# In the woven half, TensorE adds a pick two slabs behind its dot product instead of three

## The chip, the cores and the metric

One core of one Trainium2 chip. Five engines work from their own instruction queues and meet in semaphores: PE (TensorE, the matrix multiplier), DVE (VectorE), ACT (ScalarE), POOL (GpSimd) and SP (SyncE, which here only issues DMAs). The metric is the device time of one execution in microseconds (us), the median of several runs.

## The reference, cut to what matters

Two transformer blocks over 512 tokens of width 1024, the second one with 16 meta tokens ahead of them. The first block ends in a mixture of very many tiny experts: each token picks 8 heads x 16 = 128 of 16384 experts, and each expert is a row `u` and a row `v`.

```python
def chunk(args):                       # 128 tokens at a time
    hc, ec, gc = args
    u_sel = jnp.take(u, ec, axis=0)
    act = jax.nn.gelu(jnp.einsum('chkd,cd->chk', u_sel, hc), approximate=False) * gc
    v_sel = jnp.take(v, ec, axis=0)
    return jnp.einsum('chk,chkd->cd', act, v_sel)
...
for l in range(DEPTH):                 # the second block
    h = h + 0.5 * swiglu(rmsnorm(h, ffn1_norm[l]), ...)
    h = h + hybrid_mixer(rmsnorm(h, mix_norm[l]), pos, k_top, ...)   # retention and attention
    h = h + 0.5 * swiglu(rmsnorm(h, ffn2_norm[l]), ...)
```

The first 256 tokens of the second block do not need the experts of the last 256 tokens of the first block (everything is causal). The kernel uses this.

## The kernel before, in words

**Slabs.** All weights are streamed in slabs of 128 x 1024 numbers (0.5 MB each). SP loads a slab, ACT rounds it (`slabs_rounded`, L1452), DVE makes the remainder (`slabs_remainder`, L2279), and PE multiplies it in three products of reduced precision (L715), so a slab of 8 tiles is 24 matmuls. The rounded slabs have 4 places. So ACT can round slab t+3 only when PE's first matmul on slab t has ended.

**Picks.** The experts of one tile of 128 tokens are handled as 128 picks. Pick n means: one row of `u` and `v` for each of the 128 tokens. POOL gathers these 128 rows of 8 KB (1 MB, L3259) into one of 6 places (`SLOTS`), DVE takes the dot product of the `u` half with the token (L2578), ACT makes gelu, coefficient and a 128 x 128 diagonal of coefficients (L1742, L1746, L1753), and PE multiplies the diagonal with the `v` half and accumulates in two PSUM banks (`weigh`, L1068, two matmuls, which the profile shows as four). That frees the place for pick n+6. There are 4 tiles, 512 picks.

**Two halves.** Picks 0 to 255 run by themselves (to about 1440 us in the trace). Picks 256 to 511 are woven into the second block's work on its first 272 tokens, which has 261 slabs (`BLOCK2`). In this woven half every third pick is added by DVE in place of PE (`by_dve`, L2734, no diagonal). I count slabs of the woven half with t = 0 to 260. Its stages are: up and gate slabs of the first feed-forward (t = 0 to 43, in pairs), its down slabs (t = 44 to 67, three to an output chunk: 8, 8 and 6 tiles), the index and retention slabs (68 to 128), the retention output (129 to 144), the attention values (145 to 152), the attention heads (153 to 176, three slabs to a head: query, key, gate), the two output projections (177 to 192), then the second feed-forward (193 on).

**What sets the order.** Nothing is scheduled at run time. Each engine's program walks the slabs, and at each slab t it does its share of the picks up to a number that `woven_by` gives:

- `woven_by(t)` is t + 4, and one more for each five slabs of the mixer: about one pick a slab, 1.2 in the mixer.
- DVE, at its step t: the remainder of slab t+3, the dot products up to `woven_by(t)`, its own rows up to `woven_by(t - 2)` (`rows_by`), and only then what it does for the stage itself.
- ACT, at its step t: it rounds slab t+3, then makes gelu, coefficient and diagonal up to `woven_by(t - 1)`.
- PE, ahead of slab t (`slab`): `weigh` up to `added_by(t)`, which before the change is `woven_by(t - 3)`.
- Where PE would wait for DVE in a norm or ahead of an attention head's scores, `fill(2)` and `fill(1)` let it weigh up to `woven_by(t - 2)` or `woven_by(t - 1)` there. They name their own distance, so the default that is changed does not reach them.

PE runs its queue strictly in order. A `weigh` whose diagonal is not ready holds up all that stands behind it. A claim of a PSUM bank stands ahead of the `weigh` of the same slab (`one(x, 0, T, claim(gm))`: the claim is an argument and is worked out first).

**Turns.** `TURN` holds the two slabs at which the sums of a tile of tokens are taken out of PSUM, by DVE at step `TURN[i]` (L2750) and step `TURN[i] + 2` (L2586), by PE at slab `TURN[i] + 2` (`turn_rows`). PE starts the next tile's picks at `TURN[0] + 3`.

Of the kernel before, what the change touches and what calls it, by code (L numbers as in the profile page):

```python
# [181 lines left out]
BLOCK2 = 4 * FT + 2 * 3 * KT + 5 + 12 * RET_HEADS + 6 * KT + 3 * ATT_HEADS  # L182
# [15 lines left out]
def woven_by(t):  # L198

    if t < 0:  # L200
        return 0
    mixing = min(max(t + 1 - UP_AND_DOWN, 0), BLOCK2 - 2 * UP_AND_DOWN)
    return min(WOVEN, t + 4 + mixing // 5)


def turn_after(n):

    return next(t for t in range(BLOCK2) if woven_by(t - 3) >= n)


TURN = (turn_after(PICKS), turn_after(WOVEN))
assert TURN[1] + 4 < BLOCK2, TURN


def added_by(t, behind=3):

    n = woven_by(t - behind)
    return PICKS if n > PICKS and t < TURN[0] + 3 else n
# [115 lines left out]
def build(nc, slabs_d, xT_d, memT_d, metaT_d, vecs_d, consts_d, consts16_d, subk_d, wi_d, peer_uv_d, out_d,  # L334
          n_slabs):
    ctx = ExitStack()
    with ctx:
# [344 lines left out]
        def _(pe):  # L682
# [425 lines left out]
            def fill(behind=2):  # L1108


                if place[0] < BLOCK2:
                    weigh_to(added_by(place[0], behind))
# [9 lines left out]
            def slab():  # L1122

                t = place[0]
                place[0] += 1
                if t < BLOCK2:
                    weigh_to(added_by(t))
                    if t in (TURN[0] + 2, TURN[1] + 2):
                        turn_rows(list(sums_at), [acc.take(), acc.take()])
                return Slab()  # L1130
# [2290 lines left out]
```

## Time and profile before

| | us |
|---|---|
| median of 3 runs | 3600.69 |
| lowest and highest run | 3599.6, 3603.47 |
| the profiled execution, first to last instruction | 3601.5 |
| PE busy, DVE busy, ACT busy | 3316.3, 2554.4, 1537.0 |
| PE idle between 1440 and 2622 us by named waits, largest: the norms' sums (L802) | 14.4 |

The profile gives the profiled execution as its span alone; no other time of it is told, and the span lies inside the spread of the runs. A busy PE is not a PE at its peak: its matmuls overlap, and a matmul's start is shown some 0.4 us early when a pick stands ahead of it. The profile also shows the share of TensorE's clock that the chip granted (PEclk, 1.00 is 2.4 GHz, 0.50 is 1.2 GHz).

### The profile page before, as it was taken

What the parts mean: (1) busy time and instruction counts of PE and PEld (TensorE: products, weight loads), DVE (VectorE), ACT (ScalarE), POOL (GpSimd) and SP (SyncE); (2) the same over time, 40 slices, a digit from 0 to 9 for tenths busy, and PEclk for the clock granted to TensorE, in tenths of its full rate; (3) what the DMA queues carried; (4) which work ended last, traced back from release to release, by engine and by line L of the source; (5) the groups of instructions that cost most, each with busy time, mean ns of one, the idle gap of its engine ahead of it and who ended that gap; (6) DMA issues with size and microseconds to landing.
All of it is one profiled execution on the core that took longest, in us unless ns stands there. A gap on an engine that the chain in (4) does not pass through costs nothing.

```text
span 3601.5 us, 50492 instructions
## 1 busy us (share of the span) xinstructions
PE 3316.3 (92%) x18706; PEld 2633.5 (73%) x18706; DVE 2554.4 (71%) x4532; ACT 1537.0 (43%) x3089; POOL 770.5 (21%) x577
## 2 busy tenths in 40 slices
PE   7998889979898777799999999989999999999998
PEld 6886669855463222688777777767899988998898
DVE  6997143676777877687767777877867576768665
ACT  3222234245443333454444444545445443444443
POOL 1001236123435666122122122222200000000000
PEclk9999999999999999899899999999999999999999
DMA  3332224569999999699888899879956844453455
GB/s 123 94 95 75 75 83 141 182 272 397 407 415 421 417 411 418 261 377 389 324 321 312 305 372 385 317 296 341 374 176 188 267 141 131 133 184 106 140 184 156
DMA packets 184174, 918.82 MB, mean 255 GB/s; under 512 B 21536, under 2 KB 26912, under 8 KB 118128
## 3 DMA queue, kind: packets, MB, share of 16 engines
q0 software_dynamic: 73728, 536.90, 37.4%
q1 hardware_dynamic: 99248, 358.66, 29.9%
q10 hardware_dynamic: 10960, 20.12, 1.8%
q8 instruction: 145, 2.38, 0.3%
q14 instruction: 93, 0.76, 0.1%
HBM read 907.80 MB, written 7.80 MB: 254 GB/s over the span
## 4 chain that ended last, share of the span: by engine, by line
PE 72%; DVE 9%; DMA 7%; issue 5%; ACT 4%; POOL 2%; ACTq 0%; DVEq 0%; POOLq 0%
PE psum L715 54%; PE psum L1068 11%; DMA buffer_float<-in_peer_uv,buffer_uint 7%; DVE buffer_bfloat L2578 2%; POOL buffer_float L3259 2%; PE psum L1289 1%; ACT slabs_rounded L1452 1%; PE psum L723 1%; DVE buffer_float32r L2185 1%; PE psum L1274 1%; DVE norm_recip_root L2193 1%; DVE slabs_remainder L2279 1%; PE psum L1286 1%; PE psum L1372 1%; PE psum L1336 1%
## 5 line engine op out<-in xcount | busy, mean ns | idle before, releaser
L715 PE MATMUL psum<-buffer_float32r,slabs_rounded 128*128 128x256 f32 (+2 forms) x9568 | 2005.4, 309 | 70.3 <-POOL slabs_remainder L3244 30.1
L715 PEld LDWEIGHTS psum<-buffer_float32r,slabs_rounded 128*128 128x128 f32 x9568 | 1556.1, 192 | 217.3 <-issue 113.5
L715 PE MATMUL psum<-buffer_float32r,slabs_remainder 128*128 128x256 f32 (+2 forms) x4784 | 1439.8, 301 | 0.0
L2279 DVE TENSOR_TENSOR slabs_remainder<-raw_slabs,slabs_rounded 128x1024 fp32r<-128x1024 f32 x601 | 732.8, 1223 | 452.2 <-ACT slabs_rounded L1452 434.1
L1452 ACT ACTIVATE slabs_rounded<-raw_slabs 128x1024 fp32r<-128x1024 f32 x662 | 695.7, 1055 | 698.5 <-PE psum L715 620.7
L1068 PE MATMUL psum<-buffer_float,buffer_float 128*128 128x512 f32 x1712 | 825.2, 612 | 137.8 <-ACT buffer_float L1753 124.5
L715 PEld LDWEIGHTS psum<-buffer_float32r,slabs_remainder 128*128 128x128 f32 x4784 | 918.1, 192 | 29.8
L3259 POOL DMA_INDIRECT buffer_float<-in_peer_uv,buffer_uint x512 | 623.2, 1217 | 1330.8 <-PE psum L1068 753.6
L2578 DVE CUSTOM_DVE_ANT_0 buffer_bfloat<-buffer_float,buffer_float 128x1024 bf16<-128x1024 f32 x512 | 625.3, 1221 | 169.5 <-DMA buffer_float<-in_peer_uv,buffer_uint 160.8
L1068 PEld LDWEIGHTS psum<-buffer_float,buffer_float 128*128 128x128 f32 x1712 | 304.3, 193 | 519.6 <-issue 509.7
L1742 ACT ACTIVATE buffer_float<-buffer_float 128x1 f32<-128x1 f32 x512 | 100.3, 196 | 368.5 <-DVE buffer_float L2578 366.6
L3244 POOL TENSOR_TENSOR slabs_remainder<-raw_slabs,slabs_rounded 128x1024 fp32r<-128x1024 f32 x61 | 147.2, 2425 | 496.4 <-ACT slabs_rounded L1452 496.1
L1753 ACT ACTIVATE buffer_float<-fixed,buffer_float 128x128 f32<-128x128 f32 x428 | 172.1, 402 | 40.6 <-ACT buffer_float L1746 1.9
L715 PE MATMUL psum<-slabs_rounded,buffer_float32r 128*128 128x512 f32 (+1 forms) x608 | 184.2, 388 | 4.0 <-issue 4.0
L1436 ACT ACTIVATE buffer_float32r<-buffer_float 128x256 fp32r<-128x256 f32 (+3 forms) x224 | 104.0, 482 | 134.9 <-DVE buffer_float L2239 44.5
L2323 DVE SCALAR_TENSOR_TENSOR buffer_float<-buffer_float,vecs,buffer_float 128x512 f32<-128x512 f32 x232 | 158.9, 744 | 0.0
L1746 ACT ACTIVATE buffer_float<-buffer_float,buffer_float 128x1 f32<-128x1 f32 x512 | 150.9, 295 | 16.8
L2185 DVE TENSOR_TENSOR buffer_float32r<-buffer_float,buffer_float32r 128x256 fp32r<-128x256 f32 (+2 forms) x224 | 124.1, 568 | 19.8 <-ACT buffer_float32r L1436 18.1
L715 PEld LDWEIGHTS psum<-slabs_rounded,buffer_float32r 128*128 128x128 f32 x608 | 110.7, 190 | 36.4 <-issue 16.4
L715 PE MATMUL psum<-slabs_remainder,buffer_float32r 128*128 128x512 f32 (+1 forms) x304 | 113.3, 373 | 0.0
L2734 DVE SCALAR_TENSOR_TENSOR buffer_float<-buffer_float,buffer_float,buffer_float 128x1024 f32<-128x1024 f32 x82 | 105.0, 1281 | 0.0
L1837 ACT ACTIVATE buffer_float<-psum 128x256 f32<-128x256 f32 (+1 forms) x88 | 34.0, 386 | 103.4 <-PE psum L715 103.4
(213 smaller groups left out, 2039.0 us busy)
## 6 DMA issues: line engine op xcount, KB each, us to landing
raw_slabs<-in_slabs SPq DMA_DIRECT2D x682, 512.0 KB
buffer_float<-in_peer_uv,buffer_uint POOLq DMA_INDIRECT x512
buffer_float<-kept ACTq DMA_DIRECT2D x4, 874.5 KB, 6.0
xT<-in_xT ACTq DMA_DIRECT2D x4, 512.0 KB, 5.7
buffer_float<-in_consts ACTq DMA_DIRECT2D x8, 256.0 KB
kept<-buffer_float ACTq DMA_DIRECT2D x4, 512.0 KB
buffer_float<-kept ACTq DMA_DIRECT2D x2, 875.0 KB, 6.7
kept<-buffer_float ACTq DMA_DIRECT2D x4, 272.0 KB
```

Of the source, the lines that this page charges most:

```text
L715: m = pe.matmul(out, a, b, start=start and j == 0, stop=stop and j == 2)
L1068: m = pe.matmul(psum[:, b, :], diag[:, slot, :], uv_rows[slot][:, D + q * 512:D + (q + 1) * 512], start=p == 0, stop=p == PICKS - 1)
L1452: act.activation(slab_h[:, j, :], raw[:, r, :], ACT.Copy).then_inc(slab_rounded, 1)
L1746: act.activation(coefs[:, slot:slot + 1], acts[:, slot:slot + 1], ACT.Copy, scale=gates[:, tt, p:p + 1])\
L1753: act.activation(diag[:, slot, :], ident[:, :], ACT.Copy, scale=coefs[:, slot:slot + 1])\
L2185: dve.tensor_tensor(dst, src, high.bitcast(F32), ALU.subtract).then_inc(split, 1)
L2279: dve.tensor_tensor(slab_l[:, r, :], raw[:, r, :], slab_h[:, j, :].bitcast(F32), ALU.subtract)\
L2323: step(dve.scalar_tensor_tensor(out=acc, in0=cfp[:, h, t:t + S], scalar=w, in1=acc, op0=ALU.mult, op1=ALU.add))
L2578: dve.tensor_tensor_reduce(dump, uv_rows[slot][:, 0:D], hrow[tt], 1.0, 0.0, ALU.mult, ALU.add, dots[:, slot:slot + 1]).then_inc(dotted, 1)
L2734: ins = dve.scalar_tensor_tensor(out=out_rows, in0=v, scalar=c, in1=out_rows, op0=ALU.mult, op1=ALU.add)
L3244: pool.tensor_tensor(slab_l[:, r, :], raw[:, r, :], slab_h[:, j, :].bitcast(F32), ALU.subtract)\
L3259: pool.indirect_dma_start(uv_rows[slot], None, peer_uv_d, bass.IndirectOffsetOnAxis(eidx[:, tt, p:p + 1], 0))\
```

## The change

PE's distance goes from three slabs to two, in `added_by`, and the two turns are worked out from the same distance.

```diff
 def turn_after(n):

-    return next(t for t in range(BLOCK2) if woven_by(t - 3) >= n)
+    return next(t for t in range(BLOCK2) if woven_by(t - 2) >= n)
...
-def added_by(t, behind=3):
+def added_by(t, behind=2):

     n = woven_by(t - behind)
     return PICKS if n > PICKS and t < TURN[0] + 3 else n
```

`TURN` goes from (118, 230) to (117, 229). The programs of ACT, POOL and SP are the same in both kernels. DVE's differs only in where the turns stand. On PE each `weigh` (L1068) stands one slab earlier, except where a `fill` has put it already.

The start of the woven half on PE. The rows without a sign stand in both kernels; the L715 rows are the matmuls of a slab, L1068 the picks 256 and 257 (buffer 115 and 116 are the places that their rows lie in).

```order
 L715 MATMUL psum<-buffer_float32r,slabs_rounded 128x272 x2
 L715 MATMUL psum<-buffer_float32r,slabs_remainder 128x272
-L715 MATMUL psum<-buffer_float32r,slabs_rounded 128x272 x2
...
-L715 MATMUL psum<-buffer_float32r,slabs_remainder 128x272
 L1068 MATMUL psum<-buffer_float_115,buffer_float_103 128x512 x2
 L1068 MATMUL psum<-buffer_float_116,buffer_float_103 128x512 x2
```

Before, three slabs stand ahead of the first pick, now two: the 16 rows of one slab have gone from ahead of it to behind it.

An attention head on PE, before the change. L1372 ends the head before, the 256-wide L715 rows are the query slab and later the gate slab, the 272-wide ones the key slab, L1353 and L1358 turn the probabilities, and L1336 is the next head's scores. Buffers 111, 112 and 114 are places of picks (438, 439 and 441).

```order
L1372 MATMUL psum<-buffer_float_173,buffer_float_166 128x128
...
L715 MATMUL psum<-buffer_float32r,slabs_remainder 128x256
L715 MATMUL psum<-buffer_float32r,slabs_rounded 128x272 x2
...
L715 MATMUL psum<-buffer_float32r,slabs_remainder 128x272
L1068 MATMUL psum<-buffer_float_111,buffer_float_103 128x512 x2
L715 MATMUL psum<-buffer_float32r,slabs_rounded 128x256 x2
...
L1353 MATMUL psum<-fixed,buffer_float_179 128x128 x3
L1358 MATMUL psum<-fixed,buffer_float_179 16x128 x2
L1068 MATMUL psum<-buffer_float_112,buffer_float_103 128x512 x2
L1068 MATMUL psum<-buffer_float_114,buffer_float_103 128x512 x2
L1336 MATMUL psum<-buffer_float_171,buffer_float_170 128x144
```

The same head after the change:

```order
L1372 MATMUL psum<-buffer_float_173,buffer_float_166 128x128
...
L715 MATMUL psum<-buffer_float32r,slabs_remainder 128x256
L1068 MATMUL psum<-buffer_float_111,buffer_float_103 128x512 x2
L715 MATMUL psum<-buffer_float32r,slabs_rounded 128x272 x2
...
L1068 MATMUL psum<-buffer_float_112,buffer_float_103 128x512 x2
L715 MATMUL psum<-buffer_float32r,slabs_rounded 128x256 x2
...
L1353 MATMUL psum<-fixed,buffer_float_179 128x128 x3
L1358 MATMUL psum<-fixed,buffer_float_179 16x128 x2
L1068 MATMUL psum<-buffer_float_114,buffer_float_103 128x512 x2
L1336 MATMUL psum<-buffer_float_171,buffer_float_170 128x144
```

The first pick has moved from behind the key slab to ahead of it, the second from the fill ahead of the scores to ahead of the gate slab; the fill keeps one of its two.

## Rows read from the trace of the kernel before

**Rows 1.** The top of the page.

```profile
span 3601.5 us, 50492 instructions
```

**Rows 2.** Busy time by stretch: us, PE, PEld, DVE, ACT, POOL, PEclk, DMA share, GB/s.

```profile
1500.00:1660.00 160.00, 159.73 (x1030) 135.38 (x1029) 126.10 (x184) 78.17 (x177) 37.28 (x38) 1.00 0.98 383
2240.00:2390.00 150.00, 136.03 (x775) 106.50 (x774) 124.93 (x241) 86.04 (x185) 30.42 (x29) 0.93 0.80 298
2480.00:2622.00 142.00, 141.01 (x929) 116.83 (x928) 112.61 (x166) 70.21 (x158) 29.54 (x30) 1.00 0.91 350
```

**Rows 3.** Waits of PE, 1440 to 2622 us: total, times, longest.

```profile
PE psum L1068 <- ACT buffer_float L1753: 7.9, 4, 4.0
```

**Rows 4.** Up and gate slabs in order of time (start, us): PE, then ACT.

```profile
1603.17 1.88 PE L1068 MATMUL psum<-buffer_float,buffer_float 128*128 128x512 f32 x4
1604.48 0.81 PE L715 MATMUL psum<-buffer_float32r,slabs_rounded 128*128 128x272 f32 x2
1607.89 0.41 PE L715 MATMUL psum<-buffer_float32r,slabs_rounded 128*128 128x272 f32 x2
1610.89 1.54 PE L1068 MATMUL psum<-buffer_float,buffer_float 128*128 128x512 f32 x3
...
1605.27 1.06 ACT L1452 ACTIVATE slabs_rounded<-raw_slabs 128x1024 fp32r<-128x1024 f32 x1 [3.25 <-PE psum L715]
1606.84 0.41 ACT L1753 ACTIVATE buffer_float<-fixed,buffer_float 128x128 f32<-128x128 f32 x1
```

**Rows 5.** The start of the woven half: PE, then ACT.

```profile
1471.68 0.41 PE L715 MATMUL psum<-buffer_float32r,slabs_rounded 128*128 128x272 f32 x2
1479.49 8.01 PE L1068 MATMUL psum<-buffer_float,buffer_float 128*128 128x512 f32 x12 [4.65 <-DVE buffer_float L2819]
1486.93 0.81 PE L715 MATMUL psum<-buffer_float32r,slabs_rounded 128*128 128x272 f32 x2
...
1472.83 0.40 ACT L1753 ACTIVATE buffer_float<-fixed,buffer_float 128x128 f32<-128x128 f32 x1
1476.91 0.40 ACT L1753 ACTIVATE buffer_float<-fixed,buffer_float 128x128 f32<-128x128 f32 x1
```

**Rows 6.** Down slabs, one output chunk: PE, then ACT.

```profile
1666.90 0.82 PE L715 MATMUL psum<-buffer_float32r,slabs_rounded 128*128 128x272 f32 x2
1669.56 0.41 PE L715 MATMUL psum<-buffer_float32r,slabs_rounded 128*128 128x272 f32 x2
...
1669.26 0.40 ACT L1753 ACTIVATE buffer_float<-fixed,buffer_float 128x128 f32<-128x128 f32 x1
1672.74 0.43 ACT L1817 ACTIVATE buffer_float<-xT 128x272 f32<-128x272 f32 x1 [3.08 <-DVE xT L2833]
1674.63 0.40 ACT L1753 ACTIVATE buffer_float<-fixed,buffer_float 128x128 f32<-128x128 f32 x1
```

**Rows 7.** Attention heads in order of time: PE, ACT, DVE.

```profile
2285.99 0.42 PE L715 MATMUL psum<-buffer_float32r,slabs_rounded 128*128 128x272 f32 x2
2324.92 3.39 PE L1068 MATMUL psum<-buffer_float,buffer_float 128*128 128x512 f32 x4 [2.78 <-ACT buffer_float L1753]
...
2283.09 0.42 ACT L2015 ACTIVATE buffer_float<-buffer_float,buffer_float 128x144 f32<-128x144 f32 x1 [1.81 <-DVE buffer_float L3120]
2285.47 1.28 ACT L1742 ACT_TABLE_LOAD   x1
2286.77 0.20 ACT L1742 ACTIVATE buffer_float<-buffer_float 128x1 f32<-128x1 f32 x1
2287.39 0.41 ACT L1753 ACTIVATE buffer_float<-fixed,buffer_float 128x128 f32<-128x128 f32 x1
2301.68 0.42 ACT L2015 ACTIVATE buffer_float<-buffer_float,buffer_float 128x144 f32<-128x144 f32 x1 [5.54 <-DVE buffer_float L3120]
2355.41 0.42 ACT L2015 ACTIVATE buffer_float<-buffer_float,buffer_float 128x144 f32<-128x144 f32 x1 [4.34 <-DVE buffer_float L3120]
...
2290.35 1.22 DVE L2279 TENSOR_TENSOR slabs_remainder<-raw_slabs,slabs_rounded 128x1024 fp32r<-128x1024 f32 x1
```

**Rows 8.** The last output projection's first pick: PE, with its idle time.

```profile
2414.09 1.95 PE L1068 MATMUL psum<-buffer_float,buffer_float 128*128 128x512 f32 x4
```

**Rows 9.** Waits of DVE, 2060 to 2240 us: total, times, longest.

```profile
DVE buffer_bfloat L2578 <- DMA buffer_float<-in_peer_uv,buffer_uint: 21.7, 17, 4.7
```

## The prediction

> **What bounds the kernel now.** I read the busy time by stretch first, then PE's waits, then the instructions in order of time at each stage of the woven half. The execution spans 3601.5 us [rows 1]. PE is busy without a gap in the feed-forward stretches, 159.73 of 160 us and 141.01 of 142 us, while DVE, the next engine, has a fifth to spare [rows 2]. Only the attention stretch has room: 136.03 of 150 us. So between 1440 and 2622 us the time is PE's work plus PE's idle time plus what it loses at half clock. The change adds and removes no instruction on PE. It can only alter idle time and clock.
>
> Diagonals hardly hold PE up now: 7.9 us in 4 waits [rows 3]. How much slack is there? In the up and gate slabs [rows 4] a slab alone takes 3.0 us (1607.89 to 1610.89). A pick and a slab take 4.7 us (the pick from 1603.17; slab start to slab start is 3.4 plus 1.3), so a pick is 1.7. The slab shown at 1604.48 truly starts 0.4 later, since the pick ahead of it is still running. ACT rounds three slabs ahead at 1605.27, 0.4 us after that true start, and the diagonal made in the same step ends at 1606.84 + 0.41 = 1607.25. That is 2.4 us after the slab began. PE now takes it behind the slab after, three to five us later. After the change PE takes it behind this very slab, at 3.0 us. So of a slack of one slab and a bit, 0.5 us is left, with 0.15 us for the semaphore. Where ACT makes the diagonal in that minimum, nothing is lost. Where something stands between, each us of delay over 0.5 stalls PE, and PE's queue has the weight slabs behind it. The sum is then a search for the places where ACT's diagonal is late.
>
> **The change part by part.**
>
> *Start of the woven half, a gain.* PE reaches the fourth slab and waits 4.65 us for a PSUM bank, then adds three picks at once [rows 5]; they take 7.4 us to 1486.93 in place of 5.2, because this is half clock. With the change these picks stand ahead of the third slab (first piece of order), so ahead of that bank wait. PE is there at 1471.68; the first diagonal ends at 1473.23 (1472.83 + 0.40), the third pick's at 1477.31 (1476.91 + 0.40). It idles 1.7 us for the first and, two picks of 1.7 later, 0.6 for the other, in place of 4.65, then has the slab to do while the bank is emptied. Gain 2.3 us. If the clock also stays up, another 2.2 and some of the next slab, up to 5. Whether it does I can't read; I take 3, bounds 1 and 5.
>
> *Up and gate slabs, second feed-forward: nothing*, bounds -1 and +1, by the 0.5 us above.
>
> *Down slabs, a loss.* Here ACT's step for the first slab of a chunk stands behind the square of the last chunk's output, which waits for DVE [rows 6]. The last slab of a chunk (6 tiles) truly starts at 1666.90 + 0.4 = 1667.3 and ends at 1669.56: 2.3 us. The first diagonal ends at 1669.26 + 0.40, 2.4 us after that start; the second at 1674.63 + 0.40, 7.7 us after it, the square at 1672.74 ahead of it. After the change, from that start: 2.3 us slab, wait to 2.5 for the first diagonal, pick to 4.2, slab to 7.2, wait to 7.9. So 0.2 + 0.65 = 0.85 us in each of 7 chunks: +6. The chain to the second diagonal hangs on the last slab's start, so the wait comes back in every chunk. Bounds 0 (DVE turns out earlier) and +8.5.
>
> *Turn and retention output: nothing.* In 2060 to 2240 us DVE waits 21.7 us for gathers, 17 times [rows 9]: six places are too few for 1.2 picks a slab. A place is now freed a slab earlier, which takes most of that away and makes diagonals earlier. PE however has almost no idle time there to win back, one stall of 4.0 us apart [rows 3]. The gain of about 1 us on that stall meets small new stalls at the groups of four slabs. I take 0, bounds -4 and +4.
>
> *Attention, a loss.* After each head's exponentials ACT must round a slab and load the gelu table before its first diagonal: the exponential starts at 2283.09, the diagonal ends at 2287.39 + 0.41, 4.7 us later [rows 7]. The query slab is done at 2285.99. Before, the key slab followed at once and hid this. Now the pick stands ahead of the key slab (second and third piece of order), and PE stands still 1.9 us. Behind it on PE is the key slab, and behind that on DVE the rotation of the key, the next head's scores and the next exponential. So a loop closes: 4.7 + 0.15 to the diagonal, 1.7 the pick, 0.4 + 1.05 to ACT's next rounding, and then DVE's unbroken work from the remainder at 2290.35 to the next exponential at 2301.68, 11.3 us. That is 19.3 us a head. Now four heads take 72.3 us, 18.1 each (2283.09 to 2355.41). 1.2 us more for a head, and in the head where PE waited already, 2.78 us [rows 7], that wait moves up by a slab and grows to about 5. Five of the heads have a pick ahead of the key slab, one has not. 5 x 1.2 and some 1 more for the head that waits longest: +7. Bounds +2, if the idle 14 us of this stretch [rows 2] take most of it, and +14 (each of five heads longer by the 2.8 us of the long wait).
>
> One rule speaks to this place. The gelu table load takes 1.28 us in the row at 2285.47, and the next instruction starts at its end, 2286.77 [rows 7]. The Trainium skill, ScalarE: Activation LUTs, "What ACT_TABLE_LOAD costs", says that a switch costs about 2.66 us, a load of about 1283 ns and a drain of about 1380 ns. The trace has the load and no drain behind it, so the row decides; by the page the loop would be 1.4 us a head longer, which as an estimate from that page makes the sum 7 us larger.
>
> *Second output projection, a loss.* The pick at 2414.09 starts with hardly any idle time, just as its diagonal is ready [rows 8]. It now stands one slab, 3.0 us, earlier, and the diagonal (made behind a rounding of the merged output that waits for DVE) cannot come sooner. +3, bounds 0 and +3.3.
>
> *Norms:* `fill` has the same picks there: 0. *Second turn:* off PE's path: 0.
>
> Sum: -3 + 0 + 6 + 0 + 7 + 3 = +13 us. On the profiled 3601.5 us that is 3614.5; on the median of the runs, 0.8 lower, 3613.7. I say 3613.5.
>
> **The rivals.**
>
> *It is faster.* The freed place is the mechanism: with it gathers start a slab earlier, dot products and diagonals follow, and the new stalls never show. For it: the 21.7 us of DVE's waits [rows 9] and a DMA share of 0.98 [rows 2]. Against it: outside 2060 to 2240 us the dot product is not what makes a diagonal late, ACT's order is, and that is unchanged. It would leave the start's gain of 3 to 5, and up to 4 at the turn: 3593 us. It decides if DVE's waits for gathers, not ACT's steps, set the late diagonals.
>
> *No difference.* The attention stalls fall on idle time that is there anyway and the down slabs' chain is 0.5 us shorter than I read: -3 + 2 + 2 + 1 = +2, 3603 us. For it: 14 us of idle time in 150 [rows 2].
>
> *Much slower.* New idle time pulls the clock to half in every head. For it: the pick behind the 2.78 us wait took 3.39 us in place of 1.88 [rows 4, 7], which is half clock, and PEclk is 0.93 in this stretch [rows 2]. Each half-clock spell near such a wait doubles a pick and part of a slab, 3 us; five of them make 3628. The Trainium skill, TensorE: Matmul & The Clock Gate, Part 1, says the same in kind: the half rate is what an idle array falls back to, and activity releases it. Against it: in the rows only the longest wait has such a pick behind it, and four of the five new ones are near 1.9 us.
>
> **How the numbers follow.** Forecast 0.55, faster 0.12, no difference 0.18, much slower 0.15. About 7 us, 0.2%, is what a measurement of this kernel can tell from no change. The forecast's own range is its bounds taken together with some cancelling, 3606 to 3622. For 8 in 10 it must reach into the neighbours: 3600 to 3626. Faster by over 0.2% has 0.10, within 0.2% 0.21, slower 0.69.
>
> **What the profile after would show.** PE's waits for diagonals (L1068 on L1753) would grow from 7.9 us to 20 to 30. In the down slabs such a wait comes twice to a chunk, 0.2 and 0.7 us, so that a chunk is 0.85 us longer. In the attention heads it stands ahead of the key slab, and the exponentials lie 19 to 20 us apart. The 4.65 us ahead of the fourth slab are gone. DVE's waits for gathers around 2060 to 2240 us fall well below 21.7. Wrong I am if the down slabs show no waits (then ACT or DVE moves up with PE), or if the heads keep 18.1 us.

## The result and the profile after

| | before | after |
|---|---|---|
| median, us | 3600.69 | 3664.3 |
| lowest and highest of 5 runs | 3595.22, 3603.47 | 3661.72, 3668.86 |
| span of the profiled execution | 3601.5 | 3659.6 |

The ratio is 1.0182, with a 95% interval of 1.017 to 1.0194. The change costs 63.6 us, where I had forecast 13 and given 26 as the upper end. The direction was right and the size five times too small.

PE's waits ahead of picks, from 1440 us to the end of the woven half (1440 to 2680 us here), answer to [rows 3]. The first line is the waits for a diagonal, the second a wait for a sum bank at the turn. The columns are total, times, longest:

```profile
PE psum L1068 <- ACT buffer_float L1753: 66.6, 49, 8.1
PE psum L1068 <- DVE xT L2586: 3.6, 1, 3.6
```

The waits for a diagonal were 7.9 us in 4 times. So 58.7 us of new waits stand against a span that is 58.1 longer. The two are not the same thing: other waits shrink, so PE's idle time as a whole grows by 50.2 us, and the other 7.9 us are busy time (3324.2 us in place of 3316.3, in part picks at half clock, as below). The larger part of the loss is PE at rest ahead of picks whose diagonal is not there. The mean granted clock is the same in both executions (0.970 and 0.971). The busy time by stretch answers to [rows 2]. The second row is moved to where the same slabs now lie; the third keeps its 142 us and ends near the same slab:

```profile
1500.00:1660.00 160.00, 155.62 (x988) 130.37 (x988) 123.99 (x180) 76.28 (x174) 36.68 (x36) 1.00 0.96 373
2277.00:2441.00 164.00, 136.48 (x768) 105.92 (x767) 123.81 (x238) 86.40 (x185) 27.91 (x28) 0.92 0.73 265
2542.00:2684.00 142.00, 134.75 (x889) 111.97 (x889) 109.01 (x162) 67.61 (x153) 30.27 (x27) 1.00 0.88 334
```

PE was busy for 159.73 of 160 us in the first and 141.01 of 142 in the third; now it rests 4.4 and 7.3 us in stretches to which I had given nothing. PEclk is within 0.01 of before in all three.

The loss is made in every stage. This table is worked out from the starts of the slabs' first L715 matmuls; PE idle counts waits over 0.1 us. Each column is one execution; among the kept executions of the kernels below, stages that an edit does not touch differ by up to 3 us.

| slabs t | stage | us before, after | PE idle before, after | forecast | came |
|---|---|---|---|---|---|
| -3 to 3 | start of the weave | 421.5, 418.6 | 98.4, 96.8 | -3 | -2.9 |
| 3 to 44 | up and gate | 170.9, 175.7 | 0.3, 4.4 | 0 | +4.8 |
| 44 to 68 | down | 102.8, 113.5 | 1.9, 8.0 | +6 | +10.7 |
| 68 to 116 | index, retention | 282.0, 287.6 | 12.2, 18.3 | none made | +5.6 |
| 116 to 126 | turn | 62.8, 75.2 | 4.0, 12.5 | 0 | +12.4 |
| 126 to 153 | retention output, values | 125.8, 132.0 | 0.0, 6.6 | 0 | +6.2 |
| 153 to 177 | attention heads | 149.7, 164.4 | 13.3, 25.6 | +7 | +14.7 |
| 177 to 193 | output projections | 87.7, 90.0 | 9.9, 12.1 | +3 | +2.3 |
| 193 to 232 | second feed-forward | 158.3, 166.7 | 2.9, 9.6 | 0 | +8.4 |

Behind slab 232 some 3 us come back. Up to slab 232 the time grows by 62.2 us and PE's idle time by 51.0.

What holds the late diagonals? I followed each one from t = 3 on (waits over 0.1 us, one of them for another ACT result) back through ACT's unbroken work to the wait at its head: 49 picks, 66.1 us.

| ACT's unbroken work begins with | picks | us |
|---|---|---|
| the rounding of a slab that had not landed (L1452 behind DMA) | 22 | 21.4 |
| a head's exponential (L2015, waits for DVE) | 7 | 20.5 |
| other work of the stage: squares, roundings, roots, value copies | 13 | 10.8 |
| in the turn, a dot product behind ACT's wait for the stores of keys | 1 | 8.1 |
| the rest | 6 | 5.3 |

*An unlanded slab.* PE, then ACT, in the up and gate slabs, in order of time (start, us, the instruction, its idle time and who ended it), against [rows 4]:

```profile
1555.59 0.81 PE L715 MATMUL psum<-buffer_float32r,slabs_rounded 128*128 128x272 f32 x2
1560.87 1.96 PE L1068 MATMUL psum<-buffer_float,buffer_float 128*128 128x512 f32 x4 [1.71 <-ACT buffer_float L1753]
...
1558.76 1.06 ACT L1452 ACTIVATE slabs_rounded<-raw_slabs 128x1024 fp32r<-128x1024 f32 x1 [3.56 <-DMA raw_slabs<-in_slabs]
1560.33 0.40 ACT L1753 ACTIVATE buffer_float<-fixed,buffer_float 128x128 f32<-128x128 f32 x1
```

The slab begins at 1555.59 + 0.4. In [rows 4] ACT rounded 0.4 us after that. Here it stands idle until 1558.76, since the slab three ahead has not landed, and the diagonal behind that rounding ends 4.7 us after PE's slab began instead of 2.4. PE rests 1.71 us. How often ACT waits so, before (1440 to 2622 us) and after (1440 to 2680):

```profile
ACT slabs_rounded L1452 <- DMA raw_slabs<-in_slabs: 49.4, 29, 3.6
```

```profile
ACT slabs_rounded L1452 <- DMA raw_slabs<-in_slabs: 80.5, 32, 6.0
```

The kernel before had 29 such waits, up to 3.6 us, and only one reached PE, by 0.33 us (at 2348.59), because a whole slab lay between the diagonal and its use. In the up and gate slabs (1485 to 1660 us) these waits have also grown, from 11.7 us in 8 (2.6 the longest) to 29.1 in 11 (3.8).

*A down slab*, against [rows 6], PE, then ACT:

```profile
1672.44 0.81 PE L715 MATMUL psum<-buffer_float32r,slabs_rounded 128*128 128x272 f32 x2
1676.41 1.95 PE L1068 MATMUL psum<-buffer_float,buffer_float 128*128 128x512 f32 x4 [0.40 <-ACT buffer_float L1753]
...
1673.97 0.43 ACT L1817 ACTIVATE buffer_float<-xT 128x272 f32<-128x272 f32 x1 [3.07 <-DVE xT L2833]
1675.87 0.40 ACT L1753 ACTIVATE buffer_float<-fixed,buffer_float 128x128 f32<-128x128 f32 x1
```

The square stands ahead of rounding and diagonal as forecast, and costs 0.4 us where I had worked out 0.65. But it is late in only three chunks. In four others the rounding waits for a landing, 0.86 to 1.40 us each at PE.

*A head*, against [rows 7], PE, then ACT:

```profile
2322.67 0.48 PE L715 MATMUL psum<-buffer_float32r,slabs_rounded 128*128 128x256 f32 x2
2328.11 1.96 PE L1068 MATMUL psum<-buffer_float,buffer_float 128*128 128x512 f32 x4 [2.36 <-ACT buffer_float L1753]
...
2323.27 0.42 ACT L2015 ACTIVATE buffer_float<-buffer_float,buffer_float 128x144 f32<-128x144 f32 x1 [0.67 <-DVE buffer_float L3120]
2324.59 1.05 ACT L1452 ACTIVATE slabs_rounded<-raw_slabs 128x1024 fp32r<-128x1024 f32 x1
2325.65 1.28 ACT L1742 ACT_TABLE_LOAD   x1
2327.57 0.40 ACT L1753 ACTIVATE buffer_float<-fixed,buffer_float 128x128 f32<-128x128 f32 x1
2404.55 0.41 ACT L2015 ACTIVATE buffer_float<-buffer_float,buffer_float 128x144 f32<-128x144 f32 x1 [4.48 <-DVE buffer_float L3120]
```

From exponential to the end of the diagonal it is 4.7 us, as read. The four heads of [rows 7] take 81.3 us (2323.27 to 2404.55), 20.3 each, against 18.1 before and 19.3 forecast. Of the seven picks that PE waits for in the heads, four then run at about half clock, 3.5 to 3.8 us in place of 1.9; before it was one. That is the mechanism of the *much slower* rival, at four picks.

*The turn*, PE, then ACT:

```profile
2107.09 1.89 PE L1231 MATMUL psum<-buffer_float,fixed 128*128 128x256 f32 x8
2117.06 3.75 PE L1068 MATMUL psum<-buffer_float,buffer_float 128*128 128x512 f32 x4 [8.09 <-ACT buffer_float L1753]
...
2112.34 1.06 ACT L1452 ACTIVATE slabs_rounded<-raw_slabs 128x1024 fp32r<-128x1024 f32 x1 [11.37 <-DMA kept<-buffer_float]
2115.89 0.20 ACT L1742 ACTIVATE buffer_float<-buffer_float 128x1 f32<-128x1 f32 x1 [1.14 <-DVE buffer_float L2578]
```

ACT waits 11.37 us for the stores of the retention keys (`kept_ret`, L1960). They were issued at 2099.89 to 2100.73, behind two gathers of 2096.25 and 2097.49. The dot product follows the rounding, the diagonal follows that, and PE rests 8.09 us.

### The profile page after: what moved, and what is told of

It is laid out like the page before. It is cut to its first block, busy times and chain, and to the rows that moved or that the text cites. A ratio compares the mean times of both kernels' runs of the same rounds, so it can differ in the third digit from the quotient of the medians.

```text
span 3659.6 us, 50480 instructions
## 1 busy us (share of the span) xinstructions
PE 3324.2 (91%) x18706; PEld 2630.5 (72%) x18706; DVE 2556.5 (70%) x4532; ACT 1536.0 (42%) x3089; POOL 768.9 (21%) x577
## 4 chain that ended last, share of the span: by engine, by line
PE 63%; DMA 13%; DVE 10%; ACT 6%; issue 5%; POOL 2%; ACTq 0%; DVEq 0%; POOLq 0%
PE psum L715 46%; PE psum L1068 10%; DMA buffer_float<-in_peer_uv,buffer_uint 6%; DMA raw_slabs<-in_slabs 6%; DVE buffer_bfloat L2578 3%; ACT slabs_rounded L1452 2%; POOL buffer_float L3259 2%; PE psum L1289 1%; DVE buffer_float32r L2185 1%; ACT buffer_float L1753 1%; PE psum L723 1%; PE psum L1274 1%; DVE norm_recip_root L2193 1%; DVE buffer_float L2239 1%; ACT buffer_float L1746 1%
## 5 line engine op out<-in xcount | busy, mean ns | idle before, releaser
L715 PE MATMUL psum<-buffer_float32r,slabs_rounded 128*128 128x256 f32 (+2 forms) x9568 | 2005.4, 309 | 66.3 <-POOL slabs_remainder L3244 30.1
L715 PEld LDWEIGHTS psum<-buffer_float32r,slabs_rounded 128*128 128x128 f32 x9568 | 1553.6, 192 | 218.3 <-issue 117.2
L715 PE MATMUL psum<-buffer_float32r,slabs_remainder 128*128 128x256 f32 (+2 forms) x4784 | 1437.7, 301 | 0.0
L1452 ACT ACTIVATE slabs_rounded<-raw_slabs 128x1024 fp32r<-128x1024 f32 x662 | 695.8, 1056 | 796.9 <-PE psum L715 689.9
L1068 PE MATMUL psum<-buffer_float,buffer_float 128*128 128x512 f32 x1712 | 837.8, 619 | 198.0 <-ACT buffer_float L1753 182.7
L715 PEld LDWEIGHTS psum<-buffer_float32r,slabs_remainder 128*128 128x128 f32 x4784 | 915.4, 191 | 29.6
L1068 PEld LDWEIGHTS psum<-buffer_float,buffer_float 128*128 128x128 f32 x1712 | 305.5, 194 | 588.7 <-issue 586.2
L1753 ACT ACTIVATE buffer_float<-fixed,buffer_float 128x128 f32<-128x128 f32 x428 | 172.0, 402 | 40.6 <-ACT buffer_float L1746 1.9
L715 PE MATMUL psum<-slabs_rounded,buffer_float32r 128*128 128x512 f32 (+1 forms) x608 | 182.6, 386 | 1.0 <-issue 1.0
L715 PEld LDWEIGHTS psum<-slabs_rounded,buffer_float32r 128*128 128x128 f32 x608 | 109.8, 188 | 32.1 <-issue 12.4
L715 PE MATMUL psum<-slabs_remainder,buffer_float32r 128*128 128x512 f32 (+1 forms) x304 | 112.6, 370 | 0.0
```

What stands on the lines that cost most here:

```text
L715: m = pe.matmul(out, a, b, start=start and j == 0, stop=stop and j == 2)
L1068: m = pe.matmul(psum[:, b, :], diag[:, slot, :], uv_rows[slot][:, D + q * 512:D + (q + 1) * 512], start=p == 0, stop=p == PICKS - 1)
L1452: act.activation(slab_h[:, j, :], raw[:, r, :], ACT.Copy).then_inc(slab_rounded, 1)
L1753: act.activation(diag[:, slot, :], ident[:, :], ACT.Copy, scale=coefs[:, slot:slot + 1])\
```

## The experiments

Times are medians; the kernel before ran beside each set at 3599.2 to 3600.7 us. Two theories were to be told apart. **S:** a diagonal two slabs behind its dot product is made in ACT's step of the slab just ahead, and whatever stands in that step reaches PE. **G** (and its relative **F**): the places come free earlier, so gathers start earlier, and they crowd or reorder the transfers.

### Is the loss made on the spot?

`e1_near_ffn`, distance 2 only for the start and the first feed-forward:

```diff
-def added_by(t, behind=3):
+def added_by(t, behind=None):

-    n = woven_by(t - behind)
+    n = woven_by(t - (behind or (2 if t < 68 else 3)))
```

> The kernel before, with distance 2 for the slabs t < 68 alone (the start of the woven half and the first FFN), 3 behind them, and the turns where they were. In the traces the changed kernel's slab 68 starts 12 us later than before's (107 us less 95 of delay gathered). Theory P (the loss is made place by place, where a pick waits for its diagonal): 3611 to 3614. Rival R (slabs behind give a delay back, because a late TensorE lets the transfers get ahead): 3601 to 3605.

(The bracket in it is a slip; 12 us is what was meant.) Measured 3613.97 us, ratio 1.0039 (1.0026 to 1.0051): 14 us slower. By stage: up and gate 175.5, down 115.9, then every stage as before within 2 us (index and retention 282.0, heads 149.9). The time lies at the upper end of theory P's range.

`e2_near_heads`, the same edit with `2 if 153 <= t < 177`:

> The kernel before, with distance 2 in the 24 slabs of the attention heads alone (t = 153 to 176). The traces have the heads 14.7 us longer in the changed kernel. Theory P (made on the spot): 3612 to 3617. Rival R (the heads were longer only because the transfers came to them late, from the many slabs at distance 2 ahead of them): 3601 to 3606.

Measured 3615.63 us, ratio 1.0045 (1.003 to 1.0059). The heads take 161.3 us in place of 149.7, all else up to slab 232 stays within 2. Theory P holds in both: each of these stages makes its own loss, and the stages behind do not give it back.

### Do the earlier gathers do it?

`e3_gathers_held`, the changed kernel, with POOL held to the old timing:

```diff
                     pool.wait_ge(uv_used[slot], turn)
+                if n >= PURE + SLOTS:
+                    pool.wait_ge(slab_used, BLOCK1 + used_before(n - SLOTS - PURE) + 1)
...
+def used_before(k):
+    return next(t for t in range(BLOCK2) if added_by(t, 3) > k)
```

> The changed kernel, with each gather of the woven half held until TensorE has passed the slab at which the kernel before would have freed its place. TensorE still adds at distance 2, but no gather starts earlier than before. Theory G (the earlier gathers crowd out the slab loads, which are the larger part of the loss): ScalarE's waits for slab landings in the up and gate slabs fall from 29 back to about 12 us, and the time to 3605 to 3630. Theory D (the diagonal is simply not ready two slabs behind, whatever the transfers do): 3655 to 3668, with TensorE's waits for diagonals unchanged.

Measured 3655.73 us, ratio 1.0147 (1.0123 to 1.0171). PE's waits for diagonals and ACT's for landings, 1440 to 2675 us (its lines lie 5 later):

```profile
PE psum L1073 <- ACT buffer_float L1758: 61.7, 43, 6.4
```

```profile
ACT slabs_rounded L1457 <- DMA raw_slabs<-in_slabs: 50.6, 21, 4.9
```

ACT's waits for landings are back at 50.6 us from 80.5 (before: 49.4), yet only 8.6 us of the time come back (the two intervals just meet). Theory G has its effect right, but most of the loss is not that effect. The hold has a price of its own, too: one dot product comes late behind a held gather, and PE rests 5.0 us for it, at 1491.9. Behind that place the up and gate slabs cost nothing: PE is busy for 159.49 us of 1500 to 1660, where it was 159.73 before and 155.62 in the changed kernel, and ACT's waits for landings there are 7.9 us in place of 27.5. Over all stages 12 late diagonals stand behind a landing, for 11.4 us, in place of 22 for 21.4. So about half of what late landings cost comes from the gathers that start earlier.

`e9_diag_late` goes at theory S from the other side. PE stays at distance 3, gathers and dot products stay; ACT alone makes coefficients and diagonals one step later.

```diff
-                    coefficients(woven_by(t - 1))
+                    coefficients(woven_by(t - 2))
...
 def rows_by(t):
-    n = woven_by(t - 2)
+    n = woven_by(t - 3)
...
-            def fill(behind=2):
+            def fill(behind=3):
```

> The kernel before: TensorE adds at distance 3 and frees the places when it did, and the dot products stand where they stood, but ScalarE makes the coefficients and diagonals one step later, one slab ahead of their use in place of two; VectorE's rows one slab later with them, and the fills between the stages at distance 3. Theory S (what costs is that a diagonal is made in ScalarE's step of the slab just ahead: rounding, coefficient and diagonal then have to fit into one slab without its pick, 3.0 us): about the changed kernel's loss, 3645 to 3675, and TensorE's waits for diagonals as there. Rival F (what costs is the nearness of the gather and its dot product, or the earlier freeing): 3598 to 3615.

Measured 3690.89 us, ratio 1.0245 (1.023 to 1.0261). Waits of PE, 1440 to 2705 us:

```profile
PE psum L1068 <- ACT buffer_float L1753: 86.0, 50, 6.8
PE psum L1068 <- DVE buffer_float L2819: 9.3, 4, 5.2
```

A loss like that of the change, and larger than I expected (90 us; the rows and fills moved with it, and what they add isn't separated), without one gather started earlier. Theory F gave at most 3615 and is out. What costs is the one step between ACT's diagonal and PE's use of it, but not at every place: slabs 116 to 126 take 65.0 us here, against 62.8 before and 75.2 in the changed kernel, so the turn's loss is not made by this step alone. Elsewhere this kernel is the longer one: by 7.4 us in the down slabs, 6.8 behind the turn, 5.4 in the heads and 9.2 in the output projections.

### Is it the rounding ahead of the diagonal?

`e4_diag_first`, the changed kernel, ACT's step turned round:

```diff
-                if BLOCK1 + t + 3 < SLABS:
-                    split_ahead()
                 if t < BLOCK2:
                     coefficients(woven_by(t - 1))
+                if BLOCK1 + t + 3 < SLABS:
+                    split_ahead()
```

> The changed kernel, with ScalarE's step turned round: in each step the coefficients and diagonals come ahead of the rounding of the slab three ahead. Theory A (the diagonal is late because it stands behind a rounding that waits for a slab's landing): TensorE's waits for diagonals fall from 60 us to under 20 in the woven slabs and the time to 3605 to 3635. Rival (the diagonals wait for their gathers' dot products, or the rounding takes the diagonal's place as the late one): 3650 to 3675, with the waits moved to the slab's own.

Measured 3712.26 us, ratio 1.0303 (1.0283 to 1.0324), the slowest of all. My theory A fell in this form. Its rival named the right cause, dot products, but gave 3675 at most. ACT's waits, 1440 to 2730 us:

```profile
ACT buffer_float L1742 <- DVE buffer_float L2579: 434.8, 207, 4.6
ACT slabs_rounded L1452 <- DMA raw_slabs<-in_slabs: 1.5, 1, 1.5
```

The waits for landings are all but gone. In their place ACT stands 434.8 us for dot products (7.0 us in the changed kernel), and rounds late. The rounding has to stay where it is, since DVE's step begins with the remainder that needs it and makes the dot product only then.

### How much is landings?

`e10_light_near` halves the bytes of each gather in the woven half. The rows that it leaves are stale, so the last two tiles of tokens are summed from wrong rows. `e11_light_before` is the same edit of the kernel before.

```diff
-                pool.indirect_dma_start(uv_rows[slot], None, peer_uv_d,
+                pool.indirect_dma_start(uv_rows[slot] if n < PURE else uv_rows[slot][:, 0:D], None,
+                                        peer_uv_d if n < PURE else peer_uv_d.rearrange("n (two d) -> (n two) d", two=2),
```

> The changed kernel with half the bytes in each gather of the third and fourth query tile (0.5 MB in place of 1 MB; the value halves of the rows are left as an earlier gather left them, so the last two query tiles are summed from wrong rows). It is read against the next run, the kernel before with the same lightening. Theory L (about a third of the loss comes from slab loads that land late behind the gathers, which ScalarE's rounding waits for ahead of the diagonal: 22 of the 49 late diagonals, 21 us): the two differ by 30 to 42 us in place of 62, and no diagonal is late behind a landing. Rival (landings only happen to be the last of several things that are late): they differ by 55 to 65.

> The kernel before with the same lightening of the gathers, control of the run above. TensorE does not wait for a transfer in the woven slabs at distance 3, but its picks ahead of the weave and the start of it wait for gathers: 3560 to 3600, the same saving at either distance being taken out by the comparison.

Measured 3633.37 and 3592.4 us. They differ by 41.0 us, where the full kernels differ by 63.6: 22.6 us of the loss go with the transfers, by the intervals some 8 us more or less. ACT's waits for landings in the lightened changed kernel, 1440 to 2655 us, and PE's for diagonals:

```profile
ACT slabs_rounded L1452 <- DMA raw_slabs<-in_slabs: 5.4, 3, 2.6
```

```profile
PE psum L1068 <- ACT buffer_float L1753: 42.7, 25, 5.7
```

No late diagonal stands behind a landing any more. Up and gate take 169.5 us (170.5 in the other lightened kernel), the second feed-forward 157.9 (158.3): in these two stages nothing of the loss is left. In the down slabs 6.5 us are left, in the turn 13.5 and in the heads 17.4. Theory L holds, and its 22.6 us fit the 21.4 that I had counted from the trace.

### The heads

`e13_eight_slabs`, the changed kernel, with `behind or (3 if t in (158, 160, 163, 166, 169, 172, 173, 175) else 2)`:

> The changed kernel, with distance 3 at eight slabs of the attention heads alone (t = 158, 160, 163, 166, 169, 172, 173, 175), those whose pick waits 20.5 us in all for a diagonal behind ScalarE's copies of the turned probabilities. Theory H (these eight points make the heads' loss): the heads fall from 164 to about 152 us, the time to 3648 to 3655. Rival (the pick moved to the next slab waits there as long): 3660 to 3668.

(L2015 is the exponential; "copies" in that text is wrong.) Measured 3650.94 us, ratio 1.0151 (1.0133 to 1.0168). The heads take 149.1 us, the kernel before's 149.7. PE's waits for diagonals in them, 2275 to 2430 us, were 20.5 us in 7:

```profile
PE psum L1068 <- ACT buffer_float L1753: 4.0, 4, 2.8
```

Distance 3 at eight slabs brings back 13.4 us (11.8 if each kernel is set against the kernel before that ran beside it). Theory H holds.

### The turn

`e7_turn_only` and `e8_turn_late` swap the turns alone: `turn_after` with `woven_by(t - 2)` in the kernel before, and with `woven_by(t - 3)` in the changed one.

> The kernel before at distance 3, with the two turns one slab earlier (117 and 229) and nothing else. The changed kernel's trace has slabs 116 to 126 12.4 us longer; in them ScalarE stands 11.4 us for the stores of the retention keys, which were issued 2.4 us behind two gathers. Theory T (the turn's place sets when the gathers start that the stores stand behind): 3608 to 3614. Rival (the turn's place is nothing, the 12 us come from distance 2): 3600 to 3604.

> The changed kernel at distance 2, with the two turns at 118 and 230 as before. Theory T as in the run above: 3648 to 3656, ScalarE's wait for the stores under 4 us. Rival: 3660 to 3668, with that wait still over 8 us.

Measured 3600.34 us, ratio 0.9997 (0.9986 to 1.0007), and 3658.39 us, ratio 1.017 (1.0155 to 1.0186). The turn's place alone costs nothing that the times show. At distance 2 it is worth some 6 us by the medians, though the intervals overlap; slabs 116 to 126 take 67.8 us with the turn late, and 75.2 and 75.9 in two kernels with it early. So both of my either-ors were too simple. With the turn late ACT has no wait for the stores, but PE still waits 6.9 us for the next diagonal, behind a root that waits for DVE (L1874); it is the pick that waits 4.0 us in the kernel before. The early turn does put the wait for the stores in, alone too (2040 to 2140 us of the kernel with the turn alone):

```profile
ACT slabs_rounded L1452 <- DMA kept<-buffer_float: 7.7, 1, 7.7
PE psum L1068 <- ACT buffer_float L1753: 3.1, 1, 3.1
```

At distance 3 the spare slab takes up most of it.

`e15_turn_at_3` is the changed kernel with `3 if 116 <= t < 126 else 2`, turns early:

> The changed kernel, with distance 3 in slabs t = 116 to 125 alone, the turns still at 117 and 229. Slabs 116 to 126 are 12.4 us longer in the changed kernel. If distance 2 makes that on the spot: those slabs at 63 to 67 us and the time 3650 to 3656. If it comes from the order of the gathers and the stores of the keys, set by the turn's place and by what is in flight before slab 116: 72 to 76 us, and 3660 to 3667.

Measured 3650.3 us, ratio 1.014 (1.0123 to 1.0156), those slabs 63.7 us. So the turn's loss needs distance 2 in these slabs; the place of the turn changes which diagonal is late, and some of the size.

### A version with the distance by place

`e6_near_start`: `2 if t < 5 else 3`.

> The kernel before, with distance 2 for the slabs t < 5 alone. In the traces the changed kernel is 3.5 us ahead at the start of slab 5 and loses it, and more, in the up and gate slabs behind. If the loss is made on the spot by each pick at distance 2, the start keeps its gain: 3596 to 3599. If the lead is used up by the transfers (their backlog in the up and gate slabs), the gain is gone: 3600 to 3602.

Measured 3597.8 us, ratio 0.9996 (0.9987 to 1.0005). The median is where the first case has it, but the interval does not tell it from no change.

`e12_by_place`: `2 if t < 5 else 4 if 120 <= t < 130 or 153 <= t < 177 else 3`.

> The kernel before with the distance set by place: 2 for t < 5, 4 for t = 120 to 129 and t = 153 to 176, 3 elsewhere. If the loss comes from late diagonals alone, the waits that are left at distance 3 (4.0 us in the turn, 3.9 in the heads) go as well as the start's 3.5: 3590 to 3596. If at distance 4 the places come free too late for the gathers (17 and 4.7 us of VectorE's waits for them stand there already), a dot product is late in the diagonal's place: 3600 to 3610.

Measured 3594.02 us, ratio 0.9983 (0.9973 to 0.9993). Slabs 116 to 126 take 54.1 us in place of 62.8, slabs 126 to 153 take 130.5 in place of 125.8, and the heads stay at 150.0: there two diagonals are now late behind dot products (1.3 us) and one behind a landing (2.2 us). Distance 4 shows the same trade from its other side.

`e14_start_and_turn`: `2 if t < 5 else 4 if 120 <= t < 126 else 3`.

> The kernel before with distance 2 for t < 5, 4 for t = 120 to 125, and 3 elsewhere. The run with distance 4 also at t = 126 to 129 and in the heads had slabs 116 to 126 8.7 us shorter and slabs 126 to 153 4.7 us longer, behind late dot products. If the four slabs at distance 4 behind slab 125 made that loss: 3588 to 3592. If the gain of the turn is only pushed into the slabs behind it, wherever the distance goes back: 3593 to 3598.

Measured 3593.82 us, ratio 0.9979 (0.9971 to 0.9988). This is faster than the kernel before by 0.2%, the turn and the start together. The turn takes 57.8 us and the slabs behind it 127.6, so some of the gain is given back where the distance returns to 3, in two waits for a dot product; that is the second case of the expectation.

## Why the prediction was wrong, point by point

- **What bounds the kernel: right.** The loss is PE's idle time, the clock no part of it. The wait named (L1068 on L1753) is the one that grew. Of its size I said 20 to 30 us; it is 66.6. PE's idle time as a whole grew by 50.2 us.
- **Start of the woven half, -3: right.** It came to -2.9, and the 4.65 us are gone. PE waits 1.64 and 0.30 us for the diagonals, read as 1.7 and 0.6, and the picks run at full clock (3.67 us for two). That the value is met to 0.1 us is chance: this stretch took 418.6 to 422.1 us in the kept executions with distance 2, and 421.5 to 422.7 in those with 3.
- **Up and gate slabs and second feed-forward, nothing: this is the step that failed first.** It stands on "0.5 us of slack", read where ACT's diagonal is at its minimum. +4.8 and +8.4 us came. The minimum is right, but a landing that holds ACT's rounding back by more than the slack is now PE's wait. I looked at PE's waits in these stretches, not at ACT's (11.7 us for landings in the up and gate slabs before), and I counted the earlier gathers as a help only, though they raise these waits to 29.1 us. With the gathers held, the same slabs at distance 2 leave PE busy for 159.49 of 160 us, and with lighter gathers both stages lose nothing. The pair of lightened kernels sets the price over all stages: 22.6 us.
- **Down slabs, +6, bounds 0 to +8.5: mechanism right, but not alone.** 10.7 us came, 4.2 of it behind landings. Without late landings the forecast is met: the lightened kernels differ by 6.5 us here. The wait comes once to a chunk, not twice, at 0.4 us.
- **Turn and retention output, nothing, bounds ±4: failed most.** +12.4 and +6.2. The first half was right: the changed kernel has no DVE wait for a gather left in those slabs, against 21.7 us [rows 9]. What I drew from it was not. An earlier dot product does not help a diagonal that stands behind ACT's own stage work, or behind the 11.37 us for the stores. The one stall of 4.0 us, where I saw a gain of 1, is such a place: with the turn late it grew to 6.9. The run with distance 3 in these ten slabs gives 14.0 us of the 63.6 back.
- **Index and retention slabs:** I put no number on them. +5.6.
- **Attention, +7, bounds +2 to +14: place and mechanism right, size half.** +14.7. The loop is longer than 19.3 us, 20.3 in the four heads that I had read, and PE waits at seven picks, 2.9 us each on the mean, where I had five at 1.9. The long wait became 5.74 us, read as about 5.
- **Second output projection, +3: right**, +2.3 for both projections; the wait at its first pick is 2.96 us.
- **The rivals.** The faster case needed DVE's waits for gathers to set the diagonals; in the changed kernel ACT waits 7.0 us in all for dot products, so they do not. The half-clock case is out as the cause of the whole (0.970 against 0.971 mean clock), though the time lay beyond it; in the heads its mechanism did come, at four picks in place of one, and in the turn PEclk fell from 0.95 to 0.89. What that costs by itself no run separates.

The shape of the error: I priced a lost slab of slack by a few typical places. A better start is the sum over all the picks of how late each diagonal is against its new place, for which the trace of before has the ends. Laid over it afterwards, with each diagonal's end and 0.15 us against the start of the slab that its pick now stands ahead of, 40 of the 169 picks from t = 3 on are late, by 54.5 us together (11.9 in the down slabs, 9.0 in the turn, 17.8 in the heads). With the start's -3 that is 51.5 us, where 63.6 came. This sum is an estimate whose total fits better than its parts. It has nothing in the up and gate slabs and 1.2 us in the second feed-forward, where 4.8 and 8.4 came: the landings that the change itself made later are not in the old trace. And the start of that slab is a late deadline, for where a pick stood ahead of it, the new one takes that pick's place; against the start of that pick the same sum is 97.7 us over 61 picks. So it says where to look, and the size only roughly.

What stays open: why the kernel with the late diagonals loses 27 us more than the change (the stages are named above, the cause is not), and how the 5.3 us of the last row of the causes come about.

## What to carry to other kernels

When slack between a producer and an in-order engine is cut by a step, don't ask whether the usual case still fits; lay every producer's end from the trace over its new deadline and see which are late. Waits of the producer that cost nothing before (here ACT's for landings) are the first candidates, since the spare step is what made them free. Then ask what the change itself moves: here the earlier gathers made the landings later. And such a distance needn't be one number: a step more at the few places where the producer has other work, a step less where the consumer idles, beat both settings, here by 0.2% of the better one.

## What the runs showed of the hardware

- From 1500 to 1660 us, with a DMA share of 0.98 (383 GB/s), ACT's waits for 0.5 MB slabs came to 10.4 us in 7, the longest 2.6. With gathers that could start a slab earlier (share 0.96, 373 GB/s) they were 27.5 us in 10, the longest 3.8. Over the whole woven half, holding the 1 MB gathers back by a slab took the sum of these waits from 80.5 to 50.6 us; halving the gathers took it to 5.4.
- Three stores issued 2.4 to 3.2 us behind the second of two gathers had the last of them landed 11.6 us after its issue. With the turn one slab later, at the same distance, ACT has no such wait.
- The pick behind 8.09 us of rest took 3.75 us, about twice the usual 1.9. Behind the seven rests in the heads, those of 5.74, 3.20, 3.20 and 2.71 us (at 2347.63) were followed by picks of 3.75, 3.75, 3.54 and 3.65 us, those of 2.71 (at 2291.53), 2.36 and 0.54 us by picks of 1.95 and 1.96. So in the heads a rest of 3.2 us or more left PE at half clock each time, and rests of 2.7 us went either way.
